# RWKV-7 recurrence in chunks: the inverses of a step made whole ahead of its chain, results written to off-diagonal quarters of TensorE, evictions joined by direction

## What is computed

```
def step(state, inp):                       # state: 64x64 for each head
    r_t, w_t, k_t, v_t, kk_t, a_t = inp
    sa = einsum('bhvk,bhk->bhv', state, -kk_t)
    state = state * w_t[:, :, None, :] + sa[..., None] * (kk_t * a_t)[:, :, None, :] + v_t[..., None] * k_t[:, :, None, :]
    return state, einsum('bhvk,bhk->bhv', state, r_t)
y = scan(forwards) + scan(backwards)        # then a normalisation of each head, a bonus and a gate
```

## Time and profile before

| | us |
|---|---|
| median of 3 runs | 1199.62 |
| the runs | 1198.23 to 1199.64 |
| span of the profiled execution (first to last instruction) | 1183.8 |

### The profile page before, as it was taken

The page is one execution under the profiler, slowest core; times in us unless marked ns, Lnnn a source line. Parts: engine busy times, 40 slices in busy tenths (PEclk is TensorE's granted clock), DMA queues, the critical chain, the costliest instruction groups (busy, mean ns, idle before and its releaser), DMA issues. The chain is left out here.

```text
span 1183.8 us, 23882 instructions
## 1 busy us (share of the span) xinstructions
PE 1136.2 (96%) x9610; PEld 630.5 (53%) x9610; DVE 559.3 (47%) x1361; ACT 309.9 (26%) x793; POOL 254.2 (21%) x330
## 2 busy tenths in 40 slices
PE   6999999999999889889999999999899999999997
PEld 5534444444444457679895455664444444455553
DVE  4349526799969465556783444563111111111111
ACT  5054123522230377744451212300000000000000
POOL 0200410030000133633300001242345511112211
PEclk9989999999999999999999999999999999999999
DMA  9320343151220373436634841359999999777333
GB/s 342 97 51 26 104 140 87 36 178 36 89 54 36 90 188 103 132 102 179 162 90 178 286 180 72 134 210 414 406 349 336 381 337 343 293 285 293 136 135 114
DMA packets 109704, 213.19 MB, mean 180 GB/s; under 512 B 36516, under 2 KB 72836, under 8 KB 105752
## 3 DMA queue, kind: packets, MB, share of 16 engines
q1 hardware_dynamic: 81480, 127.19, 30.8%
q0 software_dynamic: 20192, 52.99, 13.7%
q10 hardware_dynamic: 7920, 31.46, 7.7%
HBM read 182.43 MB, written 35.58 MB: 184 GB/s over the span
## 5 line engine op out<-in xcount | busy, mean ns | idle before, releaser
L526 PE MATMUL pj_ps<-hT,pj_w 128*128 128x512 f32 x576 | 253.8, 597 | 0.0
L526 PEld LDWEIGHTS pj_ps<-hT,pj_w 128*128 128x128 f32 x576 | 108.2, 191 | 136.0 <-issue 135.4
L1464 PE MATMUL ps_out<-w_out,mixT 128*128 128x512 f32 x256 | 112.3, 594 | 2.1 <-PEq L2693 1.8
L2309 PE MATMUL ex_py<-wd,ex_hT 128*128 128x512 f32 x256 | 113.1, 592 | 0.0
L2458 ACT ACTIVATE ex_sg<-ex_pg 128x512 f32<-128x512 f32 x16 | 9.6, 597 | 272.8 <-PE ex_pg L2363 272.8
L738 DVE RECIPROCAL mixT<-mixT 128x1024 f32<-128x1024 f32 (+1 forms) x11 | 68.9, 6262 | 24.2 <-ACT mixT L658 19.2
L1464 PEld LDWEIGHTS ps_out<-w_out,mixT 128*128 128x128 f32 x256 | 47.8, 190 | 59.5 <-issue 59.4
L2377 PE MATMUL ex_pu<-proj 128*128 128x512 f32 x176 | 78.2, 592 | 0.0
L2363 PE MATMUL ex_pg<-proj 128*128 128x512 f32 x176 | 77.6, 594 | 0.0
L2572 DVE TENSOR_TENSOR ex_hid<-ex_pu,ex_sg 128x512 f32<-128x512 f32 x16 | 11.1, 691 | 136.1 <-PE ex_pu L2377 136.1
L2309 PEld LDWEIGHTS ex_py<-wd,ex_hT 128*128 128x128 f32 x256 | 47.1, 190 | 52.8 <-issue 52.8
(11 more groups left out here) (374 smaller groups left out, 1963.1 us busy)
## 6 DMA issues: line engine op xcount, KB each, us to landing
wd<-in_moe_w_down ACTq DMA_DIRECT2D x15, 2048.0 KB, 10.2
proj<-in_moe_w_gate SPq DMA_DIRECT2D x11, 2048.0 KB, 10.6
proj<-in_moe_w_up SPq DMA_DIRECT2D x11, 2048.0 KB, 12.2
mixT<-in_moe_w_gate SPq DMA_DIRECT2D x5, 2048.0 KB, 10.8
mixT<-in_moe_w_up SPq DMA_DIRECT2D x5, 2048.0 KB, 9.9
pj_w<-in_w_in SPq DMA_DIRECT2D x18, 512.0 KB, 4.0
proj<-in_x SPq DMA_DIRECT2D x16, 512.0 KB, 10.5
products<-pj_unit POOLq DMA_DIRECT2D x4, 2048.0 KB, 9.3
```

What stands on the lines that cost most here:

```text
L526: mm = pe.matmul(ps[:, t % 2, half, :], w_tile(t)[:, n, :], s.hT[:, n, half * 512:(half + 1) * 512], start=(n == 0), stop=(n == KD - 1))
L1464: mm = pe.matmul(s.ps_out[:, t % 2, half * 512:(half + 1) * 512], s.mixT[:, k, t * P:(t + 1) * P], s.w_out[:, k, half * 512:(half + 1) * 5 ...
L2309: mm = pe.matmul(py[:, half, :], hT[:, j, :], wd[e % 2][:, j, half * 512:(half + 1) * 512], start=(j == 0), stop=(j == KF - 1))
```

## The change

- **The inverse is made whole, ahead of the chain.** For step i + 1, during step i, TensorE forms rest = I - (transposed inverse times the part below the diagonal blocks) and from it full = rest·Tdiag, the inverse of the whole 64x64 system. VectorE transposes the loaded 32x32 blocks (`flip_inverses`) and subtracts from the identity (`rest_of_identity`), ScalarE copies `full`. The chain has W, its copy, U = full·W, its copy, and STATE. FIRST, LOW and their evictions are gone.
- **Identity blocks go.** `make` forms two rows of two blocks, 64x128 for each head, all four units in a row and before the chain's second half. The two transposed factors come from `turn`, a product with an identity constant, and ScalarE copies them unmasked (128x512, `copy_turned`). A mask covers both units of a direction (128x512).
- **Y goes to off-diagonal quarters** (head 0 to partitions 64 to 127 and the other way round), in an order that alternates one product of Y with one of STATE, and at the end with `rest_of` of the next step, both on diagonal quarters. `rwkv_out` exchanges the heads back.
- **Evictions by direction:** W, U and Y of two units in one instruction of 128x128 each.
- **The scaled old state** is computed by GpSimd (4 tensor_scalar of 128x64 a step) and no more by ScalarE.
- **Queues:** SyncE issues 2 loads of factors, 2 of exchanged factors (direction 0) and 4 of inverses (32 partitions by 4 units of 128 B each, 16 KB); GpSimd issues 2 loads of exchanged factors (direction 1) and the piece of w_out. The inverses' layout in DRAM is changed for that, and `couplings` writes in step order. The mask constants shrink from 2 x 384 to 2 x 256 columns.

The core of the diff (of `scan`; names as in the listing above, NU = 4):

```diff
+def load_exchanged(eng, s, i, d):
+    for h in range(2):
+        exchanged = s.exchanged[i % 3][(1 - h) * HD:(2 - h) * HD, 2 * d:2 * d + 2, 1:4, :].rearrange("p n f t -> p n (f t)")
+        eng.dma_start(exchanged, factors(s, i, d, h, 1)).then_inc(s.exchanged_in[d][i % 3], 16)
 def load_inverses(sp, s, i):
     for q, (h, half) in enumerate(HALVES):
-        for d in range(2):
...
+        matrix = (h * NCH + i) * 2 + half
+        src = bass.AP(s.t_dram.tensor, matrix * SIDE * SIDE, [[SIDE, SIDE], [HALF_P * SIDE * SIDE, len(UNITS)], [1, SIDE]])
+        sp.dma_start(s.ring[q * SIDE:(q + 1) * SIDE, i % 4, :, half * SIDE:(half + 1) * SIDE], src).then_inc(s.ring_in[i % 4], 16)
...
         def _(sp):
             for i in range(2, NCH):
                 if i >= 3:
-                    sp.wait_ge(y_sum, NU * (i - 2))
+                    sp.wait_ge(y_sum, 2 * (i - 2))
                 load_products(sp, s, i)
+                load_exchanged(sp, s, i, 0)
                 if i >= 4:
-                    sp.wait_ge(u_sum, NU * (i - 3))
+                    sp.wait_ge(full_sum, i - 3)
                 load_inverses(sp, s, i)
-                load_piece(i - 2)
         def _(pool):
+            scale_state(0)
             for i in range(2, NCH):
                 if i >= 3:
-                    pool.wait_ge(prods, NU * (i - 2))
-                load_exchanged(pool, s, i)
+                    pool.wait_ge(turned, i - 2)
+                load_exchanged(pool, s, i, 1)
+                load_piece(i - 2)
+                scale_state(i - 1)
+            scale_state(NCH - 1)
         def _(pe):
+            def make(i):          # waits: both loads of step i, masked of step i - 1
+                for n in range(NU):
+                    for p0, p1 in HEADS:
+                        pe.matmul(ps[p0:p1, MADE, n * P:(n + 1) * P]..., straight[p0:p1, n, 0, :], straight[p0:p1, n, 1:3, :], start=True, stop=True)
+                    for h, (p0, p1) in enumerate(HEADS):
+                        q0, q1 = HEADS[1 - h]
+                        mm = pe.matmul(ps[p0:p1, MADE + 1, n * P:(n + 1) * P]..., exchanged[q0:q1, n, 3, :], exchanged[q0:q1, n, 1:3, :], start=True, stop=True)
+                mm.then_inc(made, 1)
+            def output(i, n, m):
+                for h, (p0, p1) in enumerate(HEADS):
+                    q0, q1 = HEADS[1 - h]
+                    mm = pe.matmul(ps[q0:q1, OUTPUT + d, p * HD:(p + 1) * HD], left[p0:p1, :], right[p0:p1, :], start=(m == 0 and n % 2 == 0), stop=(m == 2 and n % 2 == 1))
+            for i in range(NCH):
+                more = i + 1 < NCH
+                for d in range(2):
+                    residuals(i, d)      # W of two units; waits masked and s_out of the direction
+                inverses(i)              # full; waits rest_out, ring_in
+                if more:
+                    make(i + 1)
+                for d in range(2):
+                    solutions(i, d)      # U; waits w_out, full_out
+                if more:
+                    turn(i + 1)
+                outputs = [(2 * d + p, m) for d in range(2) for m in range(3) for p in range(RW_PAIRS)]
+                for at, (n, m) in enumerate(outputs):
+                    output(i, n, m)
+                    if at < 2 * NU:
+                        state(i, at // 2, at % 2)
+                    elif more:
+                        rest_of(i + 1, at - 2 * NU)   # waits flipped, copied, masked of step i + 1
         def _(dve):
             for i in range(NCH):
                 statistics(i)
                 if i + 1 < NCH:
                     mask(i + 1, 0)
                     mask(i + 1, 1)
+                    flip_inverses(i + 1)
                 for n in range(NU):
+                    state(i, n)
                 if i + 1 < NCH:
+                    rest_of_identity(i + 1)
+                for d in range(2):
+                    output(i, d)
         def _(act):
+            copy_turned(0)
             for i in range(NCH):
+                for d in range(2):
+                    act.activation(pair(w, d), chain_pair(d, W), ACT.Copy).then_inc(w_out, 1)
+                act.activation(full..., ps[:, TURNED, FULL:FULL + NU * HD], ACT.Copy).then_inc(full_out, 1)
+                for d in range(2):
+                    act.activation(pair(u, d), chain_pair(d, U), ACT.Copy, scale=-1.0).then_inc(u_out, 1)
+                if i + 1 < NCH:
+                    copy_turned(i + 1)
                 statistics(i)
```

More of the change, by code:

```diff
@@ new lines, in rest_of, with inverses @@
+            def rest_of(i, n):
+                if n == 0:
+                    pe.wait_ge(flipped, i + 1)
+                    pe.wait_ge(copied, i + 1)
+                    pe.wait_ge(masked, 2 * i + 2)
+                for p0, p1 in HEADS:
+                    mm = pe.matmul(ps[p0:p1, TURNED + 1, REST + n * HD:REST + (n + 1) * HD], lm[p0:p1, i % 2, 0, n, 0, :], tr[p0:p1, n, :], start=True, stop=True)
+                if n == NU - 1:
+                    mm.then_inc(rest_sum, 1)
+            def inverses(i):
+                pe.wait_ge(rest_out, i + 1)
+                pe.wait_ge(s.ring_in[i % 4], 64 * (i // 4 + 1))
+                for n in range(NU):
+                    for p0, p1 in HEADS:
+                        mm = pe.matmul(ps[p0:p1, TURNED, FULL + n * HD:FULL + (n + 1) * HD], rest[p0:p1, n, :], s.ring[p0:p1, i % 4, n, :], start=True, stop=True)
+                mm.then_inc(full_sum, 1)
@@ new lines, in residuals @@
+            def residuals(i, d):
+                f = s.units[i % 3]
+                pe.wait_ge(masked, 2 * i + d + 1)
+                pe.wait_ge(s_out, i * NU + 2 * d + 2)
+                for p in range(RW_PAIRS):
+                    n = 2 * d + p
+                    for p0, p1 in HEADS:
+                        pe.matmul(chain(n, W)[p0:p1, :], f[p0:p1, n, 1, :], st[p0:p1, n, :], start=True, stop=False)
+                    for p0, p1 in HEADS:
+                        mm = pe.matmul(chain(n, W)[p0:p1, :], lm[p0:p1, i % 2, 1, n, 0, :], vt[p0:p1, p, step_chunk(i, d), :], start=False, stop=True)
+                mm.then_inc(w_sum, 1)
@@ new lines, in solutions, with state @@
+            def solutions(i, d):
+                pe.wait_ge(w_out, 2 * i + d + 1)
+                pe.wait_ge(full_out, i + 1)
+                for n in (2 * d, 2 * d + 1):
+                    for p0, p1 in HEADS:
+                        mm = pe.matmul(chain(n, U)[p0:p1, :], full[p0:p1, n, :], w[p0:p1, n, :], start=True, stop=True)
+                mm.then_inc(u_sum, 1)
+            def state(i, n, m):
+                d, p = UNITS[n]
+                if n % 2 == 0 and m == 0:
+                    pe.wait_ge(u_out, 2 * i + d + 1)
+                    pe.wait_ge(copied, i + 1)
+                right = (u[:, n, :], vt[:, p, step_chunk(i, d), :])[m]
+                for p0, p1 in HEADS:
+                    mm = pe.matmul(chain(n, STATE)[p0:p1, :], tp[p0:p1, i % 2, m, n, :], right[p0:p1, :], start=(m == 0), stop=(m == 1))
+                if n % 2 and m:
+                    mm.then_inc(s_sum, 1)
@@ L1291, in products @@
[L1291 removed]
+                    mm = pe.matmul(ps[q0:q1, OUTPUT + d, p * HD:(p + 1) * HD], left[p0:p1, :], right[p0:p1, :], start=(m == 0 and n % 2 == 0), stop=(m == 2 and n % 2 == 1))
+                if n % 2 and m == 2:
+                    mm.then_inc(y_sum, 1)
+            make(0)
+            turn(0)
             for n in range(NU):
[L1294 removed]
+                rest_of(0, n)
             for i in range(NCH):
[L1296 removed]
```

257 lines of the change are left out of this document (116 added, 141 removed).

## The result

Slower: 1208.05 us (median of 6, 1203.01 to 1210.81) against 1198.59 (median of 6), a ratio of 1.0076 with a 95% interval of 1.0045 to 1.0108. Forecast were 1180.3 and a range of 1170 to 1192.

What follows compares the result with a forecast made beforehand. TensorE's issue was taken to bound the kernel, SyncE's queue level with it and the next bound at 5.5 us a step. The stage, 108.2 to 88.9 us, saves 19.3: 1199.6 - 19.3 = 1180.3 us, range 1170 to 1192.

Steps and rivals of the forecast that it cites:

- Sum 5.5 us, more than the engines' 4.7. The queue is late next: SyncE's queue per scan step: eight issues, 3.8 us, plus instruction fetches, 1.7 us; claimed as bound of the new scan.
- the 4.7 itself: Scan step as set by the engines: TensorE's products and the chain of copies, masks and states, 4.7 us.
- 18 packets and 1.7 fetches a step: TensorE's code fetches: 18 in twelve batches before, 1.7 a step after, each holding SyncE's queue about 1.0 us.
- TensorE's work falls from 6.0 to 4.64 us a step: Scan step: sum of TensorE's product times after removing FIRST, LOW and identity blocks and overlapping Y; 4.64 instead of 6.0 us.
- Y runs beside STATE: Last phase of a scan step: twelve Y products each run beside one of STATE or `rest_of`, 1.41 us.
- rival C: Y and STATE don't run beside each other in the scan: 6.5 us a step, 1200.6 us in all; chance 0.06.
- Durations on the other engines: Scan instructions on VectorE, ScalarE, GpSimd: transpose 0.42 us, masks 0.69, copies 0.28 to 0.60, GpSimd's scaling 0.2 to 0.46.
- SyncE's queue bounds the step: In the scan, SyncE's load issues and the fetches holding its queue set the step at 5.5 us.
- rivals D and E: Scan loads: D, late at `make`, 1204.0 us, chance 0.06; E, queue bound with longer fetches, somewhat late loads, 1190, 0.13.
- Rival B: Fetches don't hold SyncE's queue or find it idle; engines set 4.7 us a scan step, 1171.5 us; chance 0.2.
- a granted clock under 1.00 in the scan: Sign in the scan that would show the forecast wrong altogether; no size given.
- 15.8 above the span: Whole kernel: median of the runs lies 15.8 us above the profiled span, giving the base of 1199.6 us.

Runs made afterwards that it cites:

- TensorE alone: A kernel computing nothing of the layer: four streams of matmuls without a wait, the last beside 8 MB of loads; float32 64-column stream 3.54 us a block of 256.
- The version with fewer loads: Kernel after without the loads of exchanged factors from step 3 on (other data): scan 117.0 us against 126.4 and 124.9.
- bfloat16 stream: Second stream of the kernel that computes nothing of the layer: 2048 bfloat16 matmuls of 64 rows and 64 columns, one pass each; 3.57 us a block of 256.
- float32 stream: First stream of the kernel that computes nothing of the layer: 1024 float32 matmuls of 64 rows and 64 columns on four quarters; 3.54 us a block of 256.

## Why the prediction was wrong

**The step that failed: "Sum 5.5 us, more than the engines' 4.7. The queue is late next", and before it the 4.7 itself.** TensorE's step was priced as work alone. The runs put its instruction supply there: 448 records are 1.75 blocks at 4.4 to 4.5 us, 7.8 us a step, and 16 steps are 125. I counted 18 packets and 1.7 fetches a step, and charged them to SyncE's queue only; as a limit of TensorE they had no term. The sum I didn't make is the packets' pace: 80.9 / 18 = 4.5 us each in the kernel before, hence 1.75 x 4.5 = 7.9 for a step of the new one. That trace alone couldn't have proved it: with no stops in it, 4.5 is only the pace at which packets were used up, and single ones there start 3.5 us apart (580.5 and 584.0). That it lies so close to the limit of this stage is luck; the sum would have given a rival, not a certainty.

The page "Runtime: NRT & Kernel Launch" of the Trainium skill, section Instruction fetch mechanics, says that the sequencer fetches the next 16 KiB while it executes the current ones, and calls the cost "mostly hidden". The traces agree on the block, 256 instructions, and not on the cost: it is hidden only where 256 instructions last over 3.5 us (TensorE alone) to 4.5 (beside this stage's loads). I used rows 8 and 9 to say that it was hidden "for TensorE itself". They showed no stop because the kernel before takes 6.47 us for 384 records, 4.3 a block, just at the limit; they were no evidence for a shorter one.

**By its other steps:**

- *TensorE's work falls from 6.0 to 4.64 us a step.* Right in kind: busy time falls by 16 to 21 us, 1.0 to 1.3 a step.
- *Y runs beside STATE, rival C.* Right, C is out: in the new trace MATMUL records of Y (L1375) and STATE (L1364) alternate within 0.06 us, and the timeline has

```profile
579.58 0.22 PE L1364 MATMUL sc_ps<-wd 64*64 64x64 f32 x1
579.58 0.22 PE L1375 MATMUL sc_ps<-proj,wd 64*64 64x64 f32 x1
579.58 0.22 PE L1364 MATMUL sc_ps<-wd 64*64 64x64 f32 x1
579.59 0.22 PE L1375 MATMUL sc_ps<-proj,wd 64*64 64x64 f32 x1
```

- *Durations on the other engines.* Right: transpose 0.43 us (0.42 forecast), mask 0.69, copies 0.28, 0.38 and 0.60, GpSimd's scaling 0.44 (0.2 to 0.46).
- *SyncE's queue bounds the step; late loads, rivals D and E.* Wrong: the queue idles, the loads of factors land in a median of 2.9 and 4.0 us, and TensorE waits for none. Slow issues still fall together with fetches (1.20 and 1.80 for two issues that else take 0.89; all 11 single issues of over 0.85 us in the scan overlap a q8 packet, as all 21 of the kernel before do) and cost nothing.
- *Rival B* had the fetches cost nothing and came out at 1171.5, further off. No rival had TensorE stop for its own instructions.
- *The sign "a granted clock under 1.00 in the scan".* It came (0.93 and 0.96), but the order in time makes it a companion of the stops and not their cause; the last section has the times.
- *The base, "15.8 above the span".* Taken as time around the instructions, which was wrong: device time and span differ by 1.8 us (1210.81 and 1209.0); the 15.8 was the quick execution. It shifted the forecast's level and no term of the saving.

The expected gain, then, was off what sets the end, and a new bound took its place: 16 to 21 us of work removed, 512 + 512 records added, four blocks at 4.4, +17.6 at most; measured +10.7 to +17.5 in the stage, +9.5 in the medians.

## What to carry to other kernels

Price a TensorE stage twice: by its work, and by its instructions (matmuls plus weight loads, two of each for a float32 product) in blocks of 256. The pace that the instruction queue's packets have in the trace before is a first guess at the price of a block, and a measured one only where TensorE stops between them. Where 256 instructions last under that pace, merging small matmuls pays and speeding them up does not, and a resource that shows no stops before may be just under its limit. A merged product counts as saved only if it doesn't give up quarters of the array: the version with 128 columns of weights saved the records and paid them back in work.

## What was not expected of the hardware

- The pace of the supply: 3.54 us per 256 TensorE instructions with nothing beside it, 4.2 to 4.5 in the scan of the kernel after and its versions with as many instructions, 4.9 to 6.0 beside DMA traffic of about 400 GB/s.
- The clock falls at some stops. The granted clock is 1.00 over the scan of before, 0.93 and 0.96 in the two of after, at half (1.2 GHz) for 3.4 us at a time. All eight falls come within a stop of 1.9 to 3.4 us or up to 1.1 us behind it (574.17 in the stop from 572.01 to 574.23; 557.10 behind that from 553.55 to 556.03). The version with fewer loads stops as often and keeps 1.00. In the bfloat16 stream, busy 54% of the time, it stays at 0.50 for all 50 us, and the float32 stream, busy 58%, has 1.00; both take 3.5 to 3.6 us a block, so there the clock costs nothing.
- In the kernel after, TensorE goes on 1.2 to 1.6 us after its packet is in, though the packet itself takes only about 1.1. What grows beside other traffic is the time from TensorE's going on to the start of the next packet: a median of 1.1 us in the float32 stream, 1.7 in this scan (1.1 to 3.3), 2.5 to 3.7 beside 400 GB/s. What a packet waits for in that time is not shown.
